# Two output tiles' gate products moved into the retention and its norms, with two score banks and four buffers there

## The chip, the cores and the metric

The kernel runs on one core of one Trainium2 chip. The metric is the device time of one launch in microseconds (us). TensorE is called PE here, VectorE DVE, ScalarE ACT, GpSimd POOL and SyncE SP, as in the profile; PEld is TensorE's weight load.

## The reference, cut to what matters

Two blocks of two layers each run on x of 512 tokens by 1024 features, all in f32. The change is in the mixer of the second block, once in each of its two layers:

```
h = rmsnorm(x, g);  proj = h @ w_in          # q, k, v of attention and retention, conv parts, gate_pre (3 x 1024)
o_da  = rmsnorm(diff_attention(...)) * (1 - lam_init)
o_ret = rmsnorm(retention(rq, rk, rv)) * silu(r_g)      # 4 heads of 64, decay matrix per head
o_sc  = sc_b * causal_dwconv(sc_c * sc_x)
gates = sigmoid(gate_pre + b_gate)                       # 3 gates per feature
y = gates[0]*(o_da @ w_da) + gates[1]*(o_ret @ w_ret) + gates[2]*(o_sc @ w_sc)
x = x + y @ w_out
```

The gates need only h, which is there from the start of the mixer; the branch products need o_da, o_ret and o_sc.

## The kernel before, in words

Activations lie transposed, features on the 128 partitions and the 512 tokens along the free axis, so that a tensor of 1024 features is 8 tiles of 128x512. `k.tile(n)` is one such tile in SBUF, `k.bank(b)` one of the 8 banks of PSUM, each 128x512. A weight **unit** is 8 blocks of 128x128. It comes from memory into a ring (three slots of two units each, L296 on SP's queue), ACT copies it to a rounded high half `w_hi` (`split_hi`, L312) and DVE subtracts to get the low half `w_lo` (`split_lo`, L320). `product` multiplies a unit with h in three passes (hi by hi, hi by lo, lo by hi: L339, L340, L341), 24 matmuls of 128x512. Both halves are buffered for `AHEAD` = 3 units: the halves of unit n+3 can be made only when PE is done with unit n, which it reports with `unit_used`.

There is no scheduler at run time. A `Work` has one function per engine and a number of ticks; a schedule is a list of (work, tick), and every engine walks the same list in order and issues what the work has for it. Engines are tied by semaphores alone, and an instruction that waits holds all that stands behind it on its engine. `behind(lead, followers)` places a follower's tick after the lead's tick that its rule names.

The stretch of the change, in each of the two layers, is this list:

- `turn_tiles`: PE transposes the retention's two value tiles (L1778), ACT copies them.
- `retention`: 16 units u = (head, block s), with 512, 384, 256 and 128 columns for s = 0 to 3. In tick u PE makes the scores of unit u (L1802) into bank 2 + u mod 4 and then the output of unit u-2 (L1810); DVE multiplies the scores with the decay matrix into one of eight buffers (L1819, "the decay" below). Scores of unit u wait for the decay of unit u-4, the output of u-2 for the decay of u-2. ACT copies each pair of heads when it is complete (L1826).
- `short_conv`, ticks behind the retention's at u = 0, 2, 4, 6: three DVE instructions (L1853 to L1856) in each of its ticks 1 and 2.
- `diff_norms` (a `tile_norms` of four tiles), ticks behind u = 3, 7, 11, 15 and one at the end: ACT squares tile n (L1736), PE averages the square (L1729), ACT takes the root in tick n+1 (L1741, Sqrt), DVE makes the reciprocal (L1756) and scales (L1757).
- `ret_norms` (the same for the retention's two tiles, after all of it, since its first square waits for all four `diff_norms`): with a Tanh on ACT (L1738) and two more DVE instructions for the silu gate (L1762, L1763).
- `gated_branches`, 2 ticks for each of the 8 output tiles d. First ACT and DVE split the eight source tiles into halves (L1904, and `split_tiles_lo`, L556). An even tick makes three gate units into banks 2 to 4: DVE multiplies with the norm factor (L1925), ACT takes tanh (L1910), DVE makes 0.5 t + 0.5 (L1928). The odd tick makes the three branch products of one unit, 24 matmuls (L1890 to L1892), into banks 5 to 7, which DVE multiplies with the gates (L1932) and adds up (L1935, L1936).

Of the kernel before, what the change touches and what calls it, by code (L numbers as in the profile page):

```python
# [35 lines left out]
P = 128  # L36
# [16 lines left out]
SEMS = (72, 58)  # L53
# [109 lines left out]
FFN_PARTS = [6, 5]  # L163

# [1625 lines left out]
def retention(k, q, key, val, buf, values_turned):  # L1790


    scores_done, decayed, out_done, copied = (k.sem() for _ in range(4))
    units = [(h, s) for h in range(4) for s in range(TB)]
    U = len(units)

    def tensor(pe, u):
        if u < U:
            h, s = units[u]
            if u >= 4:  # L1800
                pe.wait_ge(decayed, u - 3)
            pe.matmul(k.bank(2 + u % 4)[:, 0:T - s * P], key[h // 2][HALF[h % 2], s * P:(s + 1) * P],  # L1802
                      q[h // 2][HALF[h % 2], s * P:T], start=True, stop=True).then_inc(scores_done, 1)
        if u >= 2:
            v = u - 2
            h, s = units[v]
            if v == 0:
                pe.wait_ge(values_turned, 2)
            pe.wait_ge(decayed, v + 1)
            pe.matmul(k.bank(6 + h // 2)[HALF[h % 2], s * P:T], val[h // 2][:, s * P + 64 * (h % 2):s * P + 64 * (h % 2) + 64],  # L1810
                      buf[v % 8][:, 0:T - s * P], start=(s == 0), stop=(s == TB - 1)).then_inc(out_done, 1)

    def vector(dve, u):
        if u < U:
            h, s = units[u]
            dve.wait_ge(scores_done, u + 1)
            if u >= 8:
                dve.wait_ge(out_done, u - 7)
            dve.tensor_tensor(buf[u % 8][:, 0:T - s * P], k.c(f"decay{h}")[:, 0:T - s * P],  # L1819
                              k.bank(2 + u % 4)[:, 0:T - s * P], ALU.mult).then_inc(decayed, 1)  # L1820

    def scalar(act, u):
        if u in (9, U + 1):
            j = 0 if u == 9 else 1
            act.wait_ge(out_done, 8 * (j + 1))
            act.activation(q[j], k.bank(6 + j), ACT.Copy).then_inc(copied, 1)  # L1826

    w = Work(U + 2, tensor, scalar, vector)
    w.copied, w.out_done = copied, out_done
    return w  # L1830
# [33 lines left out]
def gated_branches(k, l, first, h, factor, src, src_ready, branch, out, gt, part):  # L1864
# [5 lines left out]
    ks = [range(0, 4), range(4, 6), range(6, 8)]  # L1870

    def tensor(pe, t):
        d = t // 2
        n = first + 4 * d
        if t % 2 == 0:
            for b in range(3):
                if d >= 1:
                    pe.wait_ge(tanh_done, 3 * (d - 1) + b + 1)
                k.product(pe, k.bank(2 + b), n + b, h)
            return  # L1880
        if d >= 1:
            pe.wait_ge(read, 3 * d)
        pe.wait_ge(k.lo_ready, n + 4)
        if d == 0:
            pe.wait_ge(src_lo, DT)
        u = (n + 3) % AHEAD
        for b in range(3):
            for i in ks[b]:
                w, end = slice(i * P, (i + 1) * P), i == ks[b][-1]
                pe.matmul(k.bank(5 + b), k.w_hi[:, u, w], branch.hi(i), start=(i == ks[b][0]), stop=False)  # L1890
                pe.matmul(k.bank(5 + b), k.w_hi[:, u, w], branch.lo(i), start=False, stop=False)  # L1891
                last = pe.matmul(k.bank(5 + b), k.w_lo[:, u, w], branch.hi(i), start=False, stop=end)  # L1892
        last.then_inc(k.unit_used, 1)

    def scalar(act, t):
        d = t // 2
        n = first + 4 * d
        if t % 2:
            k.split_hi(act, n + 3 + AHEAD)
            return  # L1900
# [4 lines left out]
        else:  # L1905
            act.wait_ge(read, 3 * d)
        for b in range(3):
            k.split_hi(act, n + b + AHEAD)
            act.wait_ge(scaled, 3 * d + b + 1)
# [5 lines left out]
    def vector(dve, t):  # L1915
        d = t // 2
        n = first + 4 * d
# [4 lines left out]
        if t % 2 == 0:  # L1922
            for b in range(3):
# [3 lines left out]
            dve.wait_ge(tanh_done, 3 * (d + 1))  # L1927
            ch.then(dve.tensor_scalar(gt, gt, 0.5, 0.5, ALU.mult, ALU.add))  # L1928
            return
        dve.wait_ge(k.unit_used, n + 4)  # L1930
        for b in range(3):
            dve.tensor_tensor(part[b], gt[:, b * T:(b + 1) * T], k.bank(5 + b), ALU.mult).then_inc(read, 1)  # L1932
        k.split_lo(dve, n + 3 + AHEAD)
# [212 lines left out]
def second_block(k, l, n, act, up, const_in, lam_in, bias_dram, out):  # L2146
# [78 lines left out]
    ret = retention(k, tiles(12, 14), tiles(14, 16), tiles(16, 18), tiles(4, 12), turn.copied)  # L2225
# [17 lines left out]
    def src_ready(act, i):  # L2243
# [4 lines left out]
        else:  # L2248
            act.wait_ge(conv.done, i - 5)

    gates = gated_branches(k, l, n, h, rstd, tiles(0, 4) + tiles(12, 14) + tiles(20, 22), src_ready,
                           k.halves(28, DT), tiles(4, 12), k.tile(14, 3), tiles(17, 20))
    schedule = ticks(turn) + behind(ret, [(conv, lambda u: 2 * u), (diff_norms, lambda u: 4 * u + 3)])
# [14 lines left out]
    schedule += ticks(ret_norms) + gate_ticks[:-1] + splits[:-1] + gate_ticks[-1:] + splits[-1:] + ticks(o.early)  # L2268
# [28 lines left out]
def pack_weights(i):  # L2297
# [26 lines left out]
    for l in range(DEPTH):  # L2324
# [4 lines left out]
        for d in range(DT):  # L2329
            g += [unit(w[:, 3328 + b * D + d * P:3328 + b * D + (d + 1) * P]) for b in range(3)]  # L2330
            g.append(unit(branch[:, d * P:(d + 1) * P]))
# [68 lines left out]
```

## Time and profile before

| | |
|---|---|
| median of 3 runs | 3365.84 us (3365.09 to 3366.28) |
| time of the profiled execution | 3363.61 us |
| its span, from first to last instruction | 3361.8 us |
| PE busy | 3212.4 us (96%) |
| DVE, ACT, POOL busy | 54%, 35%, 5% |
| mean granted TensorE clock | 0.975 |

Rows of a timeline give start, duration, engine, line and operation, the number of instructions merged (x), and in square brackets how long the engine sat idle before, with what released it. A PE matmul's duration overlaps the next one's, so the pace is read from start to start. A matmul of f32 tiles that are not split shows as two instructions.

### The profile page before, as it was taken

The numbers are of one execution on the slowest core, as the hardware profiler recorded it, in microseconds if no ns is written. First come the engines' busy times: TensorE is split into PE (matmuls) and PEld (weight loads), VectorE is DVE, ScalarE is ACT, GpSimd is POOL, SyncE is SP. The second block draws the span as 40 slices with busy tenths as digits, with TensorE's granted clock in tenths as the row PEclk, the third lists the DMA queues.
The fourth block names the chain that finished last, engine by engine and source line by source line (L and its number), as shares of the span: only waits on it lengthen the run. The fifth ranks groups of instructions, "written<-read, shape, count | busy, mean of one in ns | idle before, by whom it ended". The sixth has DMA issues, their size and how long they took to land.

```text
span 3361.8 us, 42275 instructions
## 1 busy us (share of the span) xinstructions
PE 3212.4 (96%) x17384; PEld 2531.6 (75%) x17384; DVE 1821.2 (54%) x2794; ACT 1162.8 (35%) x1813; POOL 157.1 (5%) x129
## 2 busy tenths in 40 slices
PE   9999899999899889999899899999999999999999
PEld 6778778887677667888677587788877757778887
DVE  3854443343677754333476755564647675556463
ACT  4533233232433334222343323432335332333232
POOL 1221000000000010000000000100010000010000
PEclk9999889999999988999899999999999999999999
DMA  4210012222111111222211122223222112222322
GB/s 173 76 40 19 15 63 100 88 100 96 50 63 63 63 63 63 89 99 88 96 63 64 37 100 88 97 79 108 91 94 87 63 38 100 88 88 87 108 82 81
DMA packets 41563, 264.89 MB, mean 79 GB/s; under 512 B 4600, under 2 KB 4984, under 8 KB 13980
## 3 DMA queue, kind: packets, MB, share of 16 engines
q1 hardware_dynamic: 41364, 262.18, 22.9%
q8 instruction: 138, 2.26, 0.3%
q14 instruction: 53, 0.43, 0.0%
q10 hardware_dynamic: 8, 0.01, 0.0%
HBM read 260.07 MB, written 3.42 MB: 78 GB/s over the span
## 4 chain that ended last, share of the span: by engine, by line
PE 75%; DVE 9%; ACT 3%; issue 2%; DVEq 0%; ACTq 0%; POOL 0%; POOLq 0%
PE psum L339 22%; PE psum L340 22%; PE psum L341 22%; PE psum L757 2%; DVE w_lo L320 1%; PE psum L943 1%; ACT tiles L964 1%; PE psum L934 1%; DVE tiles L989 1%; DVE tiles L1694 1%; PE psum L1890 1%; PE psum L1891 1%; PE psum L1892 1%; ACT xT L818 1%; PE psum L1802 1%
## 5 line engine op out<-in xcount | busy, mean ns | idle before, releaser
L339 PE MATMUL psum<-hi,w_hi 128*128 128x512 f32 x3672 | 1477.1, 402 | 33.5 <-DVE lo L799 15.3
L340 PE MATMUL psum<-lo,w_hi 128*128 128x512 f32 x3672 | 1456.7, 397 | 0.0
L341 PE MATMUL psum<-hi,w_lo 128*128 128x512 f32 x3672 | 1455.7, 396 | 0.0
L339 PEld LDWEIGHTS psum<-hi,w_hi 128*128 128x128 f32 x3672 | 692.7, 189 | 216.1 <-issue 16.1
L320 DVE TENSOR_TENSOR w_lo<-ring,w_hi 128x1024 fp32r<-128x1024 f32 (+1 forms) x495 | 602.9, 1218 | 427.1 <-ACT w_hi L312 426.8
L312 ACT ACTIVATE w_hi<-ring 128x1024 fp32r<-128x1024 f32 (+1 forms) x495 | 505.3, 1021 | 941.3 <-PE psum L341 880.5
L340 PEld LDWEIGHTS psum<-lo,w_hi 128*128 128x128 f32 x3672 | 693.4, 189 | 169.8 <-issue 6.1
L341 PEld LDWEIGHTS psum<-hi,w_lo 128*128 128x128 f32 x3672 | 692.4, 189 | 169.6
L730 DVE SCALAR_TENSOR_TENSOR xT<-xT,psum 128x512 f32<-128x512 f32 x96 | 66.0, 688 | 240.3 <-PE psum L341 240.3
L964 ACT ACTIVATE tiles<-tiles,small 128x256 f32<-128x256 f32 (+3 forms) x176 | 95.0, 541 | 147.3 <-DVE small L989 146.6
L1570 DVE TENSOR_TENSOR tiles<-tiles 128x512 f32<-128x512 f32 x64 | 44.3, 693 | 180.6 <-ACT tiles L1562 180.6
L1562 ACT ACTIVATE tiles<-psum 128x512 f32<-128x512 f32 x64 | 38.2, 597 | 224.7 <-PE psum L341 224.7
L934 PE MATMUL psum<-tiles 128*128 128x256 f32 (+3 forms) x352 | 107.2, 432 | 0.0
L943 PEld LDWEIGHTS psum<-tiles 128*128 128x128 f32 x400 | 53.3, 194 | 67.0 <-issue 49.1
L943 PE MATMUL psum<-tiles 128*128 128x128 f32 x400 | 63.4, 290 | 40.4 <-DVE tiles L976 35.0
L957 ACT ACTIVATE tiles<-psum 128x128 f32<-128x128 f32 (+1 forms) x80 | 34.9, 436 | 178.1 <-PE psum L925 177.9
L1925 DVE TENSOR_TENSOR psum<-psum,tiles 128x512 f32<-128x512 f32 x48 | 33.6, 699 | 107.5 <-PE psum L341 107.4
L989 DVE CUSTOM_DVE_ANT_0 tiles<-psum,tiles 128x128 f32<-128x128 f32 (+3 forms) x96 | 44.8, 485 | 64.0 <-PE psum L934 63.5
L1237 PE MATMUL psum<-tiles 64*64 64x64 f32 x2496 | 78.8, 219 | 0.5 <-DVE tiles L1393 0.5
L1237 PEld LDWEIGHTS psum<-tiles 64*64 64x64 f32 x2496 | 75.3, 135 | 3.6 <-issue 1.7
L934 PEld LDWEIGHTS psum<-tiles 128*128 128x128 f32 x352 | 59.3, 199 | 22.6 <-issue 14.4
L744 POOL TENSOR_TENSOR tiles<-tiles 128x512 f32<-128x512 f32 x18 | 31.3, 1739 | 847.4 <-ACT tiles L716 847.4
(249 smaller groups left out, 2612.2 us busy)
## 6 DMA issues: line engine op xcount, KB each, us to landing
ring<-in_weights SPq DMA_DIRECT2D x211, 1024.0 KB, 4.8
ring<-in_weights SPq DMA_DIRECT2D x28, 704.0 KB, 4.0
ring<-in_weights SPq DMA_DIRECT2D x4, 896.0 KB, 4.5
ring<-in_weights SPq DMA_DIRECT2D x3, 832.0 KB, 4.4
xT<-in_x SPq DMA_DIRECT2D x8, 256.0 KB, 5.4
tiles<-bias_repeated SPq DMA_DIRECT2D x8, 256.0 KB, 7.2
out<-xT SPq DMA_DIRECT2D x8, 256.0 KB, 2.8
held<-in_const SPq DMA_DIRECT2D x1, 1344.0 KB, 7.7
```

Source lines behind the costliest of these rows:

```text
L312: act.activation(self.w_hi[:, n % AHEAD, 0:UNITS[n] * P], self.raw(n), ACT.Copy).then_inc(self.hi_ready, 1)
L320: dve.tensor_tensor(self.w_lo[:, n % AHEAD, w], self.raw(n), self.w_hi[:, n % AHEAD, w].bitcast(F32), ALU.subtract).then_inc(self.lo_ready, 1)
L339: pe.matmul(out, hi, rhs.hi(first + at), start=(at == 0), stop=False)
L340: pe.matmul(out, hi, rhs.lo(first + at), start=False, stop=False)
L341: last = pe.matmul(out, lo, rhs.hi(first + at), start=False, stop=(at == end))
L730: dve.scalar_tensor_tensor(out=k.x(t), in0=k.x(t), scalar=scale, in1=k.bank(t % nb), op0=ALU.mult, op1=ALU.add).then_inc(added, 1)
L757: ins = pe.matmul(out[:, i * w:(i + 1) * w], src[:, i * P:(i + 1) * P], weights, start=first and i == 0, stop=last and i == TB - 1)
L934: pe.matmul(s_bank[g][:, lo:hi], q[:, i * P:(i + 1) * P], key[:, lo:hi], start=True, stop=True).then_inc(scores_done, 1)
L943: last = pe.matmul(o_bank[:, 0:P], heads[h][1][:, b], probT[:, b], start=(j == 0), stop=(j == i))
L964: act.activation(prob[g][:, lo:hi], prob[g][:, lo:hi], ACT.Exp, bias=s[:, top:top + 1], scale=-1.0, accum_out=s[:, 3 + g:4 + g]).then_inc( ...
L989: dve.tensor_tensor_reduce(out=prob[g][:, span], in0=s_bank[g][:, span], in1=bias[:, end - ((i + 1) * P - first(i)):end], scale=-scale, sc ...
L1237: last = pe.matmul(out[HALF[h], to], left[HALF[h], at_chunk(c)], right[HALF[h], at_chunk(c)], start=True, stop=True)
```

## The change

The first two output tiles' six gate units become a `Work` of their own, `early_gates`, with tiles to keep the results in and banks 4 and 5. Its ticks 0 to 3 stand behind the retention's ticks 2, 6, 10 and 14, ticks 4 and 5 between the ticks of `ret_norms`. To free banks and tiles the retention keeps two score banks and four decay buffers. `gated_branches` begins with the branch products of tiles 0 and 1, one behind the other, and makes gates from tile 2 on. The weights are packed in the new order (six gate units, two branch units, then three and one as before); their number and size stay. The lengths of the two pools of semaphores go from 72 and 58 to 74 and 56.

```
@@ retention, tensor
-            if u >= 4:
-                pe.wait_ge(decayed, u - 3)
-            pe.matmul(k.bank(2 + u % 4)[:, 0:T - s * P], key[h // 2][HALF[h % 2], s * P:(s + 1) * P],
+            if u >= 2:
+                pe.wait_ge(decayed, u - 1)
+            pe.matmul(k.bank(2 + u % 2)[:, 0:T - s * P], key[h // 2][HALF[h % 2], s * P:(s + 1) * P],
@@ retention, vector
-            if u >= 8:
-                dve.wait_ge(out_done, u - 7)
-            dve.tensor_tensor(buf[u % 8][:, 0:T - s * P], k.c(f"decay{h}")[:, 0:T - s * P],
-                              k.bank(2 + u % 4)[:, 0:T - s * P], ALU.mult).then_inc(decayed, 1)
+            if u >= 4:
+                dve.wait_ge(out_done, u - 3)
+            dve.tensor_tensor(buf[u % 4][:, 0:T - s * P], k.c(f"decay{h}")[:, 0:T - s * P],
+                              k.bank(2 + u % 2)[:, 0:T - s * P], ALU.mult).then_inc(decayed, 1)
@@ new
+def early_gates(k, l, first, h, factor, gates, banks, tile_free):
+    scaled, tanh_done, made = (k.sem() for _ in range(3))
+
+    def tensor(pe, e):
+        if e >= 2:
+            pe.wait_ge(tanh_done, e - 1)
+        k.product(pe, k.bank(banks[e % 2]), first + e, h)
+
+    def scalar(act, e):
+        d, b = e // 3, e % 3
+        k.split_hi(act, first + e + AHEAD)
+        tile_free(act, e)
+        act.wait_ge(scaled, e + 1)
+        act.activation(gates[e], k.bank(banks[e % 2]), ACT.Tanh, scale=0.5,
+                       bias=k.v("b_gate", 24 * l + 8 * b + d)).then_inc(tanh_done, 1)
+
+    def vector(dve, e):
+        dve.wait_ge(k.unit_used, first + e + 1)
+        dve.tensor_tensor(k.bank(banks[e % 2]), k.bank(banks[e % 2]), factor, ALU.mult).then_inc(scaled, 1)
+        k.split_lo(dve, first + e + AHEAD)
+        dve.wait_ge(tanh_done, e + 1)
+        dve.tensor_scalar(gates[e], gates[e], 0.5, 0.5, ALU.mult, ALU.add).then_inc(made, 1)
@@ gated_branches, tensor (odd tick, branch products)
         if d >= 1:
             pe.wait_ge(read, 3 * d)
-        pe.wait_ge(k.lo_ready, n + 4)
+        pe.wait_ge(k.lo_ready, n + 1)
         if d == 0:
             pe.wait_ge(src_lo, DT)
+            pe.wait_ge(early.tanh_done, 3 * EARLY_GATES)
@@ gated_branches, scalar and vector: no gates for d < EARLY_GATES; vector, odd tick
+        if d == 0:
+            dve.wait_ge(early.made, 3 * EARLY_GATES)
         for b in range(3):
-            dve.tensor_tensor(part[b], gt[:, b * T:(b + 1) * T], k.bank(5 + b), ALU.mult).then_inc(read, 1)
+            gate = gates[3 * d + b] if d < EARLY_GATES else gt[:, b * T:(b + 1) * T]
+            dve.tensor_tensor(part[b], gate, k.bank(5 + b), ALU.mult).then_inc(read, 1)
@@ second_block
+    held = tiles(8, 12) + [k.tile(62), k.tile(22)]
+    early = early_gates(k, l, n, h, rstd, held, (4, 5), tile_free)
-    schedule = ticks(turn) + behind(ret, [(conv, lambda u: 2 * u), (diff_norms, lambda u: 4 * u + 3)])
+    schedule = ticks(turn) + behind(ret, [(conv, lambda u: 2 * u), (diff_norms, lambda u: 4 * u + 3),
+                                          (early, lambda e: 2 + 4 * e if e < 4 else T)])
-    schedule += ticks(ret_norms) + gate_ticks[:-1] + splits[:-1] + gate_ticks[-1:] + splits[-1:] + ticks(o.early)
+    schedule += [(ret_norms, 0), first_gates[4], (ret_norms, 1), first_gates[5], (ret_norms, 2)] + gate_ticks[:-1] + splits[:-1] + gate_ticks[-1:] + splits[-1:] + ticks(o.early)
```

Lines of the changed kernel stand one further down than before until the retention's end. The rows that follow are instructions in the order in which an engine holds them; a stage semaphore has a number only.

DVE in the first layer's retention, from unit 7's decay on, before (`stage0_6` is the scores' semaphore, `stage0_8` the outputs', `stage0_12` the norms' root on ACT, `stage0_14` DVE's own):

```order
L1819 TENSOR_TENSOR tiles<-held,psum 128x128 [waits stage0_6]
L1756 RECIPROCAL tiles<-tiles 128x512 [waits stage0_12]
L1757 SCALAR_TENSOR_TENSOR tiles<-tiles,small 128x512 [waits stage0_14]
L1819 TENSOR_TENSOR tiles<-held,psum 128x512 [waits stage0_8,stage0_6]
L1819 TENSOR_TENSOR tiles<-held,psum 128x384 [waits stage0_8,stage0_6]
L1819 TENSOR_TENSOR tiles<-held,psum 128x256 [waits stage0_8,stage0_6]
```

The same engine in the changed kernel, from unit 8's decay on (L1895 is the scaling of early gate 2, `stage0_23` its tanh):

```order
L1820 TENSOR_TENSOR tiles<-held,psum 128x512 [waits stage0_8,stage0_6]
L1820 TENSOR_TENSOR tiles<-held,psum 128x384 [waits stage0_8,stage0_6]
L1820 TENSOR_TENSOR tiles<-held,psum 128x256 [waits stage0_8,stage0_6]
L1895 TENSOR_TENSOR psum<-psum,tiles 128x512 [waits unit_used]
L321 TENSOR_TENSOR w_lo<-ring,w_hi 128x1024 [waits hi_ready]
L1898 TENSOR_SCALAR tiles<-tiles 128x512 [waits stage0_23]
L1820 TENSOR_TENSOR tiles<-held,psum 128x128 [waits stage0_8,stage0_6]
L1757 RECIPROCAL tiles<-tiles 128x512 [waits stage0_12]
L1758 SCALAR_TENSOR_TENSOR tiles<-tiles,small 128x512 [waits stage0_14]
L1820 TENSOR_TENSOR tiles<-tiles,psum 128x512 [waits stage0_8,stage0_6]
```

Between the 256-column and the 128-column decay of a head now stand three instructions of an early gate, the first of which waits for the end of its product on PE; the norm's reciprocal and the next head's first decay stand behind them.

ACT over the same units, before (L1826 copies the first two heads, L1736 squares, L1741 takes roots):

```order
L1826 ACTIVATE tiles<-psum 128x512 [waits stage0_8]
L1736 ACTIVATE tiles<-tiles 128x512 [waits stage0_15]
L1741 ACTIVATE tiles<-psum,common 128x512 [waits stage0_11]
L1736 ACTIVATE tiles<-tiles 128x512 [waits stage0_15]
L1741 ACTIVATE tiles<-psum,common 128x512 [waits stage0_11]
```

And in the changed kernel (L1890 is the early gates' tanh, `stage0_22` their scaling on DVE):

```order
L313 ACTIVATE w_hi<-ring 128x1024 [waits unit_used,slot_filled2]
L1890 ACT_TABLE_LOAD
L1890 ACTIVATE tiles<-psum,vec 128x512 [waits stage0_22]
L1737 ACTIVATE tiles<-tiles 128x512 [waits stage0_15]
L1742 ACT_TABLE_LOAD
L1742 ACTIVATE tiles<-psum,common 128x512 [waits stage0_11]
```

A weight split and a tanh now stand ahead of each square and root, and a table load ahead of each change between tanh and root; this group of six stands there for early gates 2 and 3.

DVE ahead of the split of the source tiles, before:

```order
L1756 RECIPROCAL tiles<-tiles 128x512 [waits stage0_18]
L1757 SCALAR_TENSOR_TENSOR tiles<-tiles,vec 128x512 [waits stage0_20]
L1762 SCALAR_TENSOR_TENSOR tiles<-tiles 128x512 [waits stage0_19]
L1763 SCALAR_TENSOR_TENSOR tiles<-tiles 128x512 [waits stage0_20]
L556 TENSOR_TENSOR lo_4893<-tiles,hi_4892 128x512 [waits stage0_22] x8
L1925 TENSOR_TENSOR psum<-psum,tiles 128x512 [waits unit_used]
```

And in the changed kernel, from early gate 5 on:

```order
L1895 TENSOR_TENSOR psum<-psum,tiles 128x512 [waits unit_used]
L321 TENSOR_TENSOR w_lo<-ring,w_hi 128x1024 [waits hi_ready]
L1898 TENSOR_SCALAR tiles<-tiles 128x512 [waits stage0_23]
L1757 RECIPROCAL tiles<-tiles 128x512 [waits stage0_18]
L1758 SCALAR_TENSOR_TENSOR tiles<-tiles,vec 128x512 [waits stage0_20]
L1763 SCALAR_TENSOR_TENSOR tiles<-tiles 128x512 [waits stage0_19]
L1764 SCALAR_TENSOR_TENSOR tiles<-tiles 128x512 [waits stage0_20]
L557 TENSOR_TENSOR lo_4895<-tiles,hi_4894 128x512 [waits stage0_25] x8
```

The second norm and the eight splits, which before stood behind nothing that needed a gate product, now stand behind the last early gate, and no gate product is left on PE between them and the first branch product.

## Rows read from the trace of the kernel before

**Rows 1.** Head of the page.

```profile
span 3361.8 us, 42275 instructions
```

**Rows 2.** Windows: length, PE, PEld, DVE, ACT, POOL busy, PEclk, DMA share, GB/s.

```profile
1876.36:1903.74 27.38, 27.38 (x82) 10.00 (x80) 23.02 (x33) 7.10 (x11) 4.84 (x4) 1.00 0.12 39
1903.74:1932.83 29.09, 21.81 (x78) 15.37 (x77) 23.12 (x23) 15.06 (x22) 0.00 (x0) 0.82 0.00 1
...
2719.57:2776.04 56.47, 49.14 (x159) 25.32 (x157) 46.15 (x55) 22.17 (x33) 4.84 (x4) 0.91 0.06 19
```

**Rows 3.** Timeline of PE, first layer's retention to branch products.

```profile
1880.46 0.49 PE L1802 MATMUL psum<-tiles 64*128 64x128 f32 x2
...
1887.18 0.48 PE L1802 MATMUL psum<-tiles 64*128 64x128 f32 x2
...
1888.38 1.12 PE L1729 MATMUL psum<-tiles,held 128*128 128x512 f32 x2
1889.44 1.12 PE L1802 MATMUL psum<-tiles 64*128 64x512 f32 x2
...
1892.27 0.70 PE L1802 MATMUL psum<-tiles 64*128 64x256 f32 x2
...
1893.90 0.48 PE L1802 MATMUL psum<-tiles 64*128 64x128 f32 x2
...
1910.30 2.08 PE L1729 MATMUL psum<-tiles,common 128*128 128x512 f32 x2 [6.56 <-ACT tiles L1736]
...
1955.33 0.40 PE L1890 MATMUL psum<-hi,w_hi 128*128 128x512 f32 x1
```

**Rows 4.** Timeline of DVE, first layer.

```profile
1887.91 3.35 DVE L1756 RECIPROCAL tiles<-tiles 128x512 f32<-128x512 f32 x1
...
1891.96 1.48 DVE L1819 TENSOR_TENSOR tiles<-held,psum 128x512 f32<-128x512 f32 x3
...
1908.78 0.75 DVE L1757 SCALAR_TENSOR_TENSOR tiles<-tiles,small 128x512 f32<-128x512 f32 x1
1915.26 3.35 DVE L1756 RECIPROCAL tiles<-tiles 128x512 f32<-128x512 f32 x1 [5.73 <-ACT tiles L1741]
...
1926.02 4.90 DVE L556 TENSOR_TENSOR lo<-tiles,hi 128x512 fp32r<-128x512 f32 x8
...
1938.80 1.88 DVE L1932 TENSOR_TENSOR tiles<-tiles,psum 128x512 f32<-128x512 f32 x3 [1.62 <-PE psum L1892]
```

**Rows 5.** Timeline of ACT, first layer.

```profile
1912.09 0.61 ACT L1736 ACTIVATE tiles<-tiles 128x512 f32<-128x512 f32 x1
1912.61 0.61 ACT L1738 ACTIVATE tiles<-tiles 128x512 f32<-128x512 f32 x1
1913.24 1.28 ACT L1741 ACT_TABLE_LOAD   x1
1914.54 1.26 ACT L1741 ACTIVATE tiles<-psum,common 128x512 f32<-128x512 f32 x2
...
1949.99 1.06 ACT L312 ACTIVATE w_hi<-ring 128x1024 fp32r<-128x1024 f32 x1 [3.94 <-PE psum L341]
1950.95 0.67 ACT L1910 ACTIVATE tiles<-psum,vec 128x512 f32<-128x512 f32 x1
1955.59 1.06 ACT L312 ACTIVATE w_hi<-ring 128x1024 fp32r<-128x1024 f32 x1 [3.97 <-PE psum L341]
```

**Rows 6.** Timeline of PE around two other waits.

```profile
911.46 0.68 PE L943 MATMUL psum<-tiles 128*128 128x128 f32 x4 [2.14 <-DVE tiles L976]
...
1779.56 0.72 PE L943 MATMUL psum<-tiles 128*128 128x128 f32 x4 [3.54 <-DVE tiles L976]
```

**Rows 7.** Windows behind the waits of rows 6 and 3, columns as in rows 2.

```profile
1910.30:1916.60 6.30, 5.92 (x9) 2.92 (x10) 1.34 (x1) 6.26 (x9) 0.00 (x0) 0.50 0.00 0
1780.00:1783.40 3.40, 3.40 (x11) 2.73 (x10) 2.43 (x8) 2.17 (x5) 0.00 (x0) 0.51 0.00 0
...
911.00:916.00 5.00, 4.54 (x22) 3.80 (x23) 2.81 (x12) 2.77 (x8) 0.00 (x0) 1.00 0.26 110
```

## What was predicted

> **What bounds the kernel now.** I read the head of the page first: a span of 3361.8 us [rows 1]; the execution took 3363.6 us, 2.2 us less than the median of the runs, 3365.8. Then windows over the stretch that the change touches, in both layers. From the turn of the values to the first branch product the first layer needs 27.4 + 29.1 = 56.5 us, the second as long [rows 2]. The first part, turn and retention, is PE's: busy 27.38 of 27.38 us [rows 2]. So a gate product put there does not fill a hole, it lengthens the part by its own 5.6 us (the pace of the weight splits, 1949.99 to 1955.59 [rows 5]). But DVE is busy there too, 23.0 of 27.4 us, with reciprocals of 3.35 us between the decays [rows 2, 4], and PE can pass them only because its scores run four units ahead. The second part is where PE loses: it waits 6.56 us for the first square of `ret_norms` [rows 3] and then runs at the granted clock of 0.50, the 1.2 GHz level, for 6.3 us [rows 7]. Its work there is two norm matmuls of 1.06 us and three products of 5.6, together 18.9, so 29.1 - 18.9 = 10.2 us per layer is all that the change can win. DVE is busy 23.1 of these 29.1 us [rows 2]: the second norm ends and the eight source splits begin at 1926.02 and last 4.9 us, and the branch product at 1932.83 comes just behind them [rows 4, 2]. The three gate products are the cover of that DVE work.
>
> **The change, step by step.** The mechanism that decides is DVE's order. The scaling of early gate e stands ahead of the last decay of its head, and waits for the whole product. Behind it are the weight split, the gate's 0.5 t + 0.5, the decay, then the norm's reciprocal and only then the next head's first decay. With two score banks PE cannot start unit u before the decay of u-2, so the next product can't start before that first decay is done. I count from P, the moment PE could start the instruction behind a product.
>
> The leg behind early gates 2 and 3: ACT begins 0.26 us after P (1955.33 to 1955.59 [rows 3, 5]) and splits for 1.06; a table load, 1.30 to the next start; tanh at 2.62; 0.52 to the square at 3.14, 0.63 to the next load at 3.77, 1.30 to the root at 5.07, 0.72 to DVE's reciprocal at 5.8 [rows 4, 5]. From its start to the next decay are 4.05 us (1887.91 to 1891.96 [rows 4]): 9.84. That decay is about 0.7 (512 of the 1152 columns of 1.48 us [rows 4] give 0.66), so PE goes on at 10.6. A unit of 256 columns with its output takes 1.63 (1892.27 to 1893.90 [rows 3]), and the next product starts at 12.2 and ends at **17.8**. Without waits it would be 1887.18 to 1893.90 = 6.7 [rows 3] plus 5.6 = 12.3.
>
> The other periods, each from the end of one product to the end of the next:
> - Turn to P0: 1876.36 to 1880.46 is 4.1 [rows 2, 3], plus 5.6: **9.7**.
> - P0 to P1: no reciprocal yet. Tanh at 0.26 + 0.96 [rows 5] = 1.22, square 1.74, its 0.61 and a lag of 0.07 to PE's norm matmul at 2.4, then 1.06 + 2.83 + 1.63 (1888.38, 1889.44, 1892.27, 1893.90 [rows 3]) + 5.6: **13.5**. The convolution's DVE instructions lie beside PE's waits and cost nothing; with that cover gone they would add 2 us.
> - P1 to P2: as the leg above, but ACT holds tanh's table, 1.4 less: **16.4**.
> - P2 to P3: **17.8**.
> - P3 to P4: no next head. Two reciprocals follow, the second at 9.84, the last scaling at 9.84 + 3.38 = 13.2, and from there to PE's norm matmul 1908.78 to 1910.30 = 1.52 [rows 4, 3]: 14.7. PE was done at about 6, so it waits 9 us, longer than the 6.56 of before, and comes back at the 1.2 GHz level: 2.08 for the norm matmul [rows 3], to 16.8, and the rest of 6.3 slow us, 4.2, does 2.1 of the 5.6 [rows 7]; 3.5 more ends at about **24.5**.
> - P4 to P5: the second square waits behind gate 4's tanh: norm matmul at 2.4, + 1.06 + 5.6 = **9.1**. DVE's first retention norm starts at 1.74 + 0.52 + 0.63 + 1.30 + 0.72 = 4.9 and needs 5.38 (half of 1915.26 to 1926.02 [rows 4]), to 10.3, which is P5 + 1.2.
> - P5 to branch 0: scaling at 1.2 to 1.9, load, tanh at 3.2, load 3.8, root 5.1, reciprocal 5.85, 5.38 to 11.2, eight splits 4.9 [rows 4] to 16.1. PE has nothing to do in all of this: **16.2**.
>
> The sum is 9.7 + 13.5 + 16.4 + 17.8 + 24.5 + 9.1 + 16.2 = 107.2 us. Three more products than before are done by then, 16.8 us which the steady part is spared: 90.4 against 56.5, **+33.9**. Then come costs behind it. Branch product 0 runs after a wait of 16 us; the slow spells in the rows last 3.4 and 6.3 us [rows 7] and half of one is lost, 1.7 to 3.1: I take 2.4. Branch product 1 stands right behind it and waits for DVE to read banks 5 to 7: 0.26 + 1.88 [rows 3, 4] + 0.05 = 2.2, which before lay under gate products. Last, the clock in the new short waits: by the periods above PE stops for 2.9 (before P2), 2.6 and 2.9 (P3), 2.6 (P4), 2.4 (P5) and 2.2 us (branch 1). A wait of 2.14 us left the granted clock at 1.00, one of 3.54 was followed by 3.4 us at 0.51, a loss of 1.7 [rows 6, 7]. Six waits between them cost 0 to 10.2; I take half, 5. That is 33.9 + 2.4 + 2.2 + 5 = 43.5 per layer, 87 for both. The span goes from 3361.8 to 3449, the execution to 3451, the median to **3453**.
>
> At nothing I cost the new order of the weights (same units, same groups, asked for at a slower pace than before, with a DMA share of 0.12 and 0.00 in these windows [rows 2]), the four decay buffers (a buffer's output, unit u-4, is issued two units earlier on PE) and the copies of L1826, which ACT makes between a root and the next split while PE runs a product. If a ring slot were late it would delay a split behind it; the pace leaves 11 us per slot.
>
> ACT's table switches: four per layer in this stretch before, ten now, and eight lie on the chain above (one behind gate 1, two each behind 2 and 3, one behind 4, two behind 5). A load is 1.28 us, the root starts 1.30 after it, and the instruction ahead of it is followed by the load as soon as its own 0.61 is over [rows 5]. The sum has them at that price, 10.4 us per layer. The Trainium skill, "ScalarE: Activation LUTs", section "What ACT_TABLE_LOAD costs", gives 1.28 us for the load and 1.38 more for draining, 2.66 for each switch; by that the sum would be 8 x 1.38 x 2 = 22 us higher, 3475. The rows show no such drain here, so I keep theirs.
>
> **The rivals.**
> - *Faster.* The gates fill PE's waits and DVE keeps pace: 2 x 10.2 us won, 3345. For it: PE truly stands idle 6.56 us and runs slow [rows 3, 7]. It decides where the way from the turn to branch 0 takes less than 56.5 + 16.8 = 73.3 us, and I get 107. DVE alone is busy 23.0 + 23.1 [rows 2], and gets three more gates at about 0.7 + 1.2 + 0.5, so it would have to lose under 20 us in waits for six products of 5.6. 3 in 100.
> - *The last wait is covered.* DVE has its norms done early enough that the 16.2 us before branch 0 and the slow clock behind it vanish: 43.5 - 16.2 - 2.4 = 24.9 per layer, 3416. Against it stands the fixed order, norm and splits behind gate 5. 8 in 100.
> - *A table switch costs more than its row.* If each of the eight held ACT as long again as the 1.30 us of the rows [rows 5], 8 x 1.3 x 2 = 21 us, 3474. 6 in 100. It is the case that the Trainium skill's page on ScalarE's tables would have.
> - *The clock stays low through the stretch.* If each of the six short waits brings a spell of 6.3 us [rows 7], 19 instead of 5 per layer, 3481. 5 in 100.
> - *No change.* The waits fall where PE was waiting anyway. 2 in 100, since PE was busy all through the retention.
>
> **How the numbers follow.** The chain as worked out has 76 in 100, with 3425 to 3470 as its own range: the clock terms at their lower ends take off 2 x (5 + 0.7), at their upper ends add 2 x (5.2 + 0.7), and some 10 us either way are for steps of the walk that are off by a few tenths each. The range 3410 to 3488 takes in the covered wait below and the two cases above. Slower 95, faster 3, within 0.2% (6.7 us, about what a measurement can tell) 2 in 100.
>
> **What the profile would show.** Right: PE idle 8 to 9 us before the first retention norm matmul and about 16 before branch product 0; waits of 2 to 3 us before tick 10's and 14's scores, released by DVE's decay; DVE idle 4 to 5 us before each L1895, released by PE; six more table loads per layer; a turn-to-branch window of 105 to 115 us; the same pace from tile 2 on. It is wrong if the decay behind a reciprocal does not release PE, if ACT's squares and roots run ahead of the tanh, or if the granted clock stays at 1.00 through the waits.

## The result, and the profile after

The changed kernel takes 3456.7 us (median of 4 runs, 3450.1 to 3458.9) against 3365.5; the ratio is 1.0271, with an interval of 1.0255 to 1.0286. It is 91 us slower, where 3453 was forecast. Of the ten runs of the kernel `both` below one took 8040 us; its ratio leaves that run out, and no trace explains it.

The page of the changed kernel, its head and its line of busy times:

```profile
span 3455.1 us, 42303 instructions
...
PE 3240.3 (94%) x17384; PEld 2545.8 (74%) x17384; DVE 1823.2 (53%) x2802; ACT 1178.9 (34%) x1825; POOL 156.8 (5%) x129
```

PE has the same 17384 instructions and is busy 28 us longer, since matmuls take longer where the granted clock is lower; the span grew by 93.3. The rest of the growth is waiting. The two layers show the same pattern; the rows below are the first layer's.

The timeline of PE in the changed kernel, the lines that answer to [rows 3]; a line without brackets had no wait ahead of it:

```profile
1888.22 0.49 PE L1803 MATMUL psum<-tiles 64*128 64x128 f32 x2
...
1890.59 1.12 PE L1730 MATMUL psum<-tiles,held 128*128 128x512 f32 x2 [1.10 <-ACT tiles L1737]
...
1901.90 0.48 PE L1803 MATMUL psum<-tiles 64*128 64x128 f32 x2
...
1911.04 0.73 PE L1803 MATMUL psum<-tiles 64*128 64x256 f32 x2 [2.81 <-DVE tiles L1820]
...
1920.01 0.48 PE L1803 MATMUL psum<-tiles 64*128 64x128 f32 x2
...
1923.80 1.13 PE L1730 MATMUL psum<-tiles,held 128*128 128x512 f32 x2 [2.52 <-ACT tiles L1737]
...
1930.57 1.22 PE L1803 MATMUL psum<-tiles 64*128 64x256 f32 x2 [0.74 <-DVE tiles L1820]
...
1940.22 0.48 PE L1803 MATMUL psum<-tiles 64*128 64x128 f32 x2
...
1954.94 2.08 PE L1730 MATMUL psum<-tiles,common 128*128 128x512 f32 x2 [9.01 <-ACT tiles L1737]
...
1966.03 1.96 PE L1730 MATMUL psum<-tiles,common 128*128 128x512 f32 x2 [2.30 <-ACT tiles L1737]
...
1989.95 0.77 PE L1937 MATMUL psum<-hi,w_hi 128*128 128x512 f32 x1 [15.57 <-DVE lo L557]
...
1999.38 0.50 PE L1937 MATMUL psum<-hi,w_hi 128*128 128x512 f32 x1 [1.98 <-DVE tiles L1985]
```

Each line of 128 columns of L1803 is the first instruction behind an early product, so the ends of products 0 to 3 are 1888.22, 1901.90, 1920.01 and 1940.22. Product 4 ends at 1966.03 - 2.30 = 1963.73 and product 5 at 1989.95 - 15.57 = 1974.38. What DVE did in the leg behind early gate 2, to set beside [rows 4]:

```profile
1920.11 0.70 DVE L1895 TENSOR_TENSOR psum<-psum,tiles 128x512 f32<-128x512 f32 x1 [7.89 <-PE psum L342]
1921.26 1.23 DVE L321 TENSOR_TENSOR w_lo<-ring,w_hi 128x1024 fp32r<-128x1024 f32 x1 [0.45 <-ACT w_hi L313]
1923.26 0.43 DVE L1898 TENSOR_SCALAR tiles<-tiles 128x512 f32<-128x512 f32 x1 [0.77 <-ACT tiles L1890]
1923.60 0.28 DVE L1820 TENSOR_TENSOR tiles<-held,psum 128x128 f32<-128x128 f32 x1
1925.78 3.35 DVE L1757 RECIPROCAL tiles<-tiles 128x512 f32<-128x512 f32 x1 [1.90 <-ACT tiles L1742]
...
1929.83 1.15 DVE L1820 TENSOR_TENSOR tiles<-tiles,psum 128x512 f32<-128x512 f32 x2
```

DVE stands still for 7.89 us until the product is over, and then PE waits in turn for what DVE has to do: reciprocal at 5.8 us behind the product, decay at 9.8, as worked out. ACT in the same leg, to set beside [rows 5]:

```profile
1920.17 1.06 ACT L313 ACTIVATE w_hi<-ring 128x1024 fp32r<-128x1024 f32 x1 [11.31 <-PE psum L342]
1921.25 1.28 ACT L1890 ACT_TABLE_LOAD   x1
1922.54 0.69 ACT L1890 ACTIVATE tiles<-psum,vec 128x512 f32<-128x512 f32 x1
1923.13 0.62 ACT L1737 ACTIVATE tiles<-tiles 128x512 f32<-128x512 f32 x1
1923.76 1.28 ACT L1742 ACT_TABLE_LOAD   x1
1925.06 0.69 ACT L1742 ACTIVATE tiles<-psum,common 128x512 f32<-128x512 f32 x1
```

Windows of the changed kernel from product to product, with the columns of [rows 2]:

```profile
1888.22:1901.90 13.68, 12.58 (x44) 6.66 (x43) 6.42 (x14) 2.15 (x3) 1.29 (x1) 1.00 0.00 0
1901.90:1920.01 18.11, 14.20 (x44) 7.25 (x43) 8.04 (x9) 4.72 (x6) 0.00 (x0) 0.91 0.17 58
1920.01:1940.22 20.21, 16.95 (x43) 7.99 (x43) 8.13 (x9) 5.51 (x6) 0.00 (x0) 0.75 0.00 1
1940.22:1963.73 23.51, 11.98 (x37) 7.28 (x36) 10.66 (x8) 9.23 (x11) 0.00 (x0) 0.78 0.13 45
1963.73:1974.38 10.65, 8.35 (x27) 5.67 (x26) 7.66 (x7) 4.64 (x6) 0.00 (x0) 0.84 0.00 0
1974.38:1989.95 15.57, 0.00 (x1) 0.03 (x1) 12.56 (x15) 9.26 (x13) 0.00 (x0) 0.57 0.19 67
1989.95:2006.61 16.66, 14.69 (x48) 11.38 (x49) 4.31 (x6) 1.06 (x1) 0.00 (x0) 0.79 0.00 1
```

The first column is the length of each period, the seventh the granted clock. From the turn to the first branch product are 112.0 us in the first layer and 113.8 in the second, against 56.5 in both before; three gate products more are done by then in each. The parts add up to the growth of the span: 55.6 + 57.3 in the two stretches, 9.9 and 11.3 less in what follows them (three products of 5.6 fewer, less what the two branch products lose), and 1.6 more ahead of the first.

### The profile page after: what moved, and what is told of

It is laid out like the page before. It is cut to its first block, busy times and chain, and to the rows that moved or that the text cites. A ratio compares the mean times of both kernels' runs of the same rounds, so it can differ in the third digit from the quotient of the medians.

```text
span 3455.1 us, 42303 instructions
## 1 busy us (share of the span) xinstructions
PE 3240.3 (94%) x17384; PEld 2545.8 (74%) x17384; DVE 1823.2 (53%) x2802; ACT 1178.9 (34%) x1825; POOL 156.8 (5%) x129
## 4 chain that ended last, share of the span: by engine, by line
PE 75%; DVE 8%; ACT 4%; issue 2%; DVEq 0%; ACTq 0%; POOL 0%; POOLq 0%
PE psum L340 22%; PE psum L342 22%; PE psum L341 22%; PE psum L758 2%; DVE w_lo L321 1%; PE psum L944 1%; PE psum L935 1%; ACT tiles L965 1%; PE psum L1937 1%; PE psum L1938 1%; PE psum L1939 1%; DVE tiles L1695 1%; DVE tiles L990 1%; ACT xT L819 1%; ACT w_hi L313 1%
## 5 line engine op out<-in xcount | busy, mean ns | idle before, releaser
L340 PE MATMUL psum<-hi,w_hi 128*128 128x512 f32 x3672 | 1484.1, 404 | 32.4 <-DVE lo L800 14.0
L1937 PE MATMUL psum<-hi,w_hi 128*128 128x512 f32 x128 | 53.5, 418 | 35.1 <-DVE lo L557 31.1
L935 PEld LDWEIGHTS psum<-tiles 128*128 128x128 f32 x352 | 59.2, 198 | 22.5 <-issue 14.3
L1974 DVE TENSOR_TENSOR psum<-psum,tiles 128x512 f32<-128x512 f32 x36 | 25.2, 699 | 92.2 <-PE psum L342 92.2
```

Of the source, the lines that this page charges most:

```text
L340: pe.matmul(out, hi, rhs.hi(first + at), start=(at == 0), stop=False)
L935: pe.matmul(s_bank[g][:, lo:hi], q[:, i * P:(i + 1) * P], key[:, lo:hi], start=True, stop=True).then_inc(scores_done, 1)
```

## The experiments

The table has the stretch from the turn to the first branch product, read from each profile's PE timeline, beside the time. All ratios are to runs of the kernel before that were made beside the kernel in question; their medians lie between 3364.1 and 3365.5, so that a ratio can differ a little from that of the two medians shown.

| kernel | median us | ratio, interval | stretch, layers 1 and 2 (us) |
|---|---|---|---|
| before | 3365.5 | | 56.5, 56.5 |
| changed | 3456.7 | 1.0271, 1.0255 to 1.0286 | 112.0, 113.8 |
| banks | 3366.8 | 1.0008, 0.9997 to 1.0018 | 57.7, 57.7 |
| late_rest | 3424.7 | 1.0175, 1.0160 to 1.0191 | 97.7, 97.3 |
| no_tanh | 3428.2 | 1.0188, 1.0173 to 1.0203 | 102.6, 101.4 |
| after_sources | 3450.5 | 1.0261, 1.0239 to 1.0283 | 108.4, 110.3 |
| pe_fill | 3370.8 | 1.0021, 1.0011 to 1.0030 | 56.5, 56.5 |
| short_chain | 3361.9 | 0.9993, 0.9983 to 1.0002 | 54.0, 55.1 |
| both | 3357.7 | 0.9978, 0.9968 to 0.9987 | 50.8, 50.8 |
| both_ahead | 3352.1 | 0.9967, 0.9956 to 0.9979 | 50.2, 50.2 |
| pool_splits | 3347.4 | 0.9951, 0.9936 to 0.9966 | 50.1, 50.0 |

The theory was that of the prediction: DVE's place in the list, ahead of the reciprocal and the next head's decay, makes PE and DVE wait for each other in turn, and the last products no longer cover DVE's chain. The rivals were the banks, the table loads, and PE's own load.

### banks

```
-            if u >= 4:
-                pe.wait_ge(decayed, u - 3)
-            pe.matmul(k.bank(2 + u % 4)...
+            if u >= 2:
+                pe.wait_ge(decayed, u - 1)
+            pe.matmul(k.bank(2 + u % 2)...
```

and the buffers 8 to 4, in the kernel before.

> The kernel before with one part of the change alone: two score banks and four decay buffers, no early gates. Theory (the gates' place in DVE's order costs the time, the banks next to nothing): PE waits 0.4 us in the first units and about 0.5 at each head whose first decay stands behind a reciprocal, 1.5 to 2 us per layer, 3369 us (3367 to 3371). Rival (the banks make PE wait for DVE at every unit and carry a good part of the 91 us): 3385 or more.

3366.8 us; the stretch is 1.2 us longer in each layer. The timeline of PE has two small waits that were not there before, besides the one ahead of the branch product:

```profile
1895.14 0.70 PE L1802 MATMUL psum<-tiles 64*128 64x256 f32 x2 [0.35 <-DVE tiles L1819]
1902.28 0.70 PE L1802 MATMUL psum<-tiles 64*128 64x256 f32 x2 [0.35 <-DVE tiles L1819]
```

The first scores take 0.4 us longer too (2.60 for 2.20). By themselves two banks and four buffers cost next to nothing: 1.2 us, where the stretch of the changed kernel grew by 55.5, and an interval of the ratio that includes 1. Beside early gates they may cost more, for with four banks PE could run further ahead of the late decay; no kernel with early gates and four banks was run.

### late_rest

In the changed kernel, `early_gates` is cut in two works, the products and the rest:

```
-    w = Work(3 * EARLY_GATES, tensor, scalar, vector)
+    w = Work(3 * EARLY_GATES, tensor)
+    w.rest = Work(3 * EARLY_GATES, scalar=scalar, vector=vector)
...
-                                          (early, lambda e: 2 + 4 * e if e < 4 else T)])
+                                          (early, lambda e: 2 + 4 * e if e < 4 else T),
+                                          (early.rest, lambda e: 4 + 4 * e if e < 4 else T)])
```

Ticks 4 and 5 keep products and rest together where they were.

> The changed kernel with its products where they are, but what DVE and ACT do for early gates 0 to 3 (scaling, weight split, tanh, 0.5 t + 0.5) set behind the next head's first decay, ticks 4, 8, 12 and 16 of the retention. Theory (DVE's wait for the product, ahead of reciprocal and decay, sets each period): a reciprocal starts 0.8 us behind a product and not 4.2 to 5.8, so the periods of 13.7, 18.1 and 20.2 us become 12.3, 12.8 and 12.8, with no clock loss, 15 to 16 us per layer, 3425 us (3419 to 3431). Rival (the six products cost PE time in a part where PE was full, wherever DVE's share stands): within 5 us of 3457.

3424.7 us, 32 less than the changed kernel. The timeline of DVE behind product 2, which ended at 1913.66:

```profile
1914.18 0.29 DVE L1820 TENSOR_TENSOR tiles<-held,psum 128x128 f32<-128x128 f32 x1 [5.12 <-PE psum L1803]
1914.39 3.35 DVE L1757 RECIPROCAL tiles<-tiles 128x512 f32<-128x512 f32 x1
...
1918.44 0.68 DVE L1820 TENSOR_TENSOR tiles<-tiles,psum 128x512 f32<-128x512 f32 x1
1919.03 0.69 DVE L1895 TENSOR_TENSOR psum<-psum,tiles 128x512 f32<-128x512 f32 x1
```

The reciprocal starts 0.7 us behind the product and not 5.8, and PE waits 0.35 us ahead of the unit of 256 columns. Products 0 to 3 end at 1888.22, 1900.74, 1913.66 and 1926.59: periods of 12.5, 12.9 and 12.9 us, where 12.3, 12.8 and 12.8 were expected. The products are the same and PE's order is the same, so in these three periods their place on PE costs little beyond their own 5.6 us each; DVE's and ACT's order does. It is 14.3 and 16.5 us per layer, of the 38.7 and 40.5 by which the changed kernel's stretches exceed 56.5 us and three products of 5.6. The rest stands as it did: the wait of 15.57 us ahead of the branch products, and the period from product 3 to 4, 22.9 us here and 23.5 before, in which PE now waits 10.49 us for the first square of the retention's norms. The order of the follow-ups does not touch these, and no run tries the second of them by itself.

### no_tanh

```
-        act.activation(gates[e], k.bank(banks[e % 2]), ACT.Tanh, scale=0.5,
+        act.activation(gates[e], k.bank(banks[e % 2]), ACT.Identity, scale=0.5,
```

> The changed kernel with ACT's Identity in place of Tanh for the six early gates, so that these gates have wrong values (a part of the computation is changed) and six of the ten table loads per layer are gone. Theory (loads lie on the chain at the 1.30 us of their rows): 2.6 us less in each of the three legs with two loads, 15.6 in all, and 0 to 6 more where a shorter wait keeps the clock up, 3438 us (3434 to 3442). Rival 1 (a switch costs 2.6 to 2.7 us with its drain): 32 less, 3425. Rival 2 (the loads are hidden in PE's waits): no change, 3457.

3428.2 us, 28 less than the changed kernel, and so past the expected 18 and near the first rival's 32. The trace tells the two apart. The ACT timeline has the leg behind early gate 2 without loads:

```profile
1918.69 1.06 ACT L313 ACTIVATE w_hi<-ring 128x1024 fp32r<-128x1024 f32 x1 [11.34 <-PE psum L342]
1919.65 0.67 ACT L1890 ACTIVATE tiles<-psum,vec 128x512 f32<-128x512 f32 x1
1920.22 0.62 ACT L1737 ACTIVATE tiles<-tiles 128x512 f32<-128x512 f32 x1
1920.74 0.68 ACT L1742 ACTIVATE tiles<-psum,common 128x512 f32<-128x512 f32 x1
```

The root starts 2.05 us behind the split and not 4.89, so two loads cost 2.84, 1.4 each with the lag at each change, and no drain of another 1.38 each. By the product ends 1900.38, 1918.53 and 1935.22 and the first branch product at 1979.06, the three legs with loads are shorter by 3.5, 3.2 and 2.5; the stretch is 9.4 us shorter in the first layer and 12.3 in the second. The two stretches give 21.7 us, of which the loads explain 6 x 1.4 x 2 = 17; the rest of these is put down to the clock (its mean over the stretches is 0.88 against 0.82), which no run separates. Of the other 7 us between the two profiled spans, 1.5 lie ahead of the first stretch and 5.2 between the stretches, where nothing was changed: from the first branch product to the next turn are 771.7 us against 776.9. The last section shows what that is. So the rival's total was nearly met and its cause is not there.

### after_sources

In the changed kernel, ACT's copies and DVE's subtractions for source tiles 0, 1, 6, 7, 2 and 3 become ticks of their own:

```
-    schedule += [(ret_norms, 0), first_gates[4], ...
+    schedule += [(ret_norms, 0)] + ticks(gates.sources) + [first_gates[4], ...
```

> The changed kernel with the splits of six of the eight source tiles moved from behind the last early gate to behind the first retention square, where DVE waits 9.6 us for a gate product and ACT 7.0. Theory (nothing covers DVE's chain ahead of the first branch product in the changed kernel, so what leaves it comes off in full): 6 x 0.61 us, the wait of 15.6 us becomes 11.9, 7 us in all, 3449 us (3446 to 3453). Rival (the first branch product waits for the last early gate's tanh or weight split as long): no change, 3457.

3450.5 us, 6 less than the changed kernel. The PE timeline:

```profile
1986.34 0.76 PE L1946 MATMUL psum<-hi,w_hi 128*128 128x512 f32 x1 [12.14 <-DVE lo L1916]
```

The wait of 15.57 is 12.14 and the stretches are 3.6 and 3.5 us shorter, six subtractions' worth. What leaves DVE's chain behind the last early gate comes off in full: nothing covers it in the changed kernel. This shows it for 3.5 of the 15.57 us; that the other 12 go the same way is argued from the chain, not tried.

### pe_fill

In the kernel before, gate product 0 moves on PE alone:

```
+    w.filler = Work(1, lambda pe, t: k.product(pe, k.bank(2), first, h))
...
-    schedule += ticks(ret_norms) + gate_ticks[:-1] ...
+    schedule += ticks(gates.filler) + ticks(ret_norms) + gate_ticks[:-1] ...
```

> The kernel before with the first gate product moved on PE alone into its wait of 6.56 us ahead of the retention's norms; nothing moves on DVE or ACT. Theory (in the second part DVE's chain of reciprocals and splits sets the start of the first branch product, so that filling PE wins nothing): the branch product starts within 0.3 us of where it did, PE waits some 6 us just ahead of it and the branch product runs at the lower clock, 2 to 3 us lost per layer: 3370 us (3365 to 3372). Rival (the wait and the slow clock are PE's to win, 5 to 9 us per layer): 3348 to 3355.

3370.8 us, 0.2% slower, with an interval that leaves out 1. The PE timeline, against [rows 3]:

```profile
1912.86 1.12 PE L1729 MATMUL psum<-tiles,common 128*128 128x512 f32 x2 [0.76 <-ACT tiles L1736]
...
1935.39 0.80 PE L1892 MATMUL psum<-hi,w_hi 128*128 128x512 f32 x1 [6.16 <-DVE w_lo L320]
```

The wait ahead of the norms goes from 6.56 to 0.76 us, and all of it comes back as 6.16 us ahead of the branch product; the stretch is 56.5 us to the tenth. The idle time that the change set out from was never PE's to win alone.

### short_chain, both, both_ahead, pool_splits

These start from the kernel before. short_chain sets the two tanh of the retention's norms behind both roots and splits six source tiles ahead of the norms:

```
+        if n == N and tanh_last:
+            for m in range(N):
+                act.activation(th[m], jobs[m][4], ACT.Tanh, scale=0.5).then_inc(tanh_done, 1)
...
-    schedule += ticks(ret_norms) + gate_ticks[:-1] ...
+    sources = ticks(gates.sources)
+    schedule += sources[:5] + [(ret_norms, 0), sources[5]] + ticks(ret_norms)[1:] + gate_ticks[:-1] ...
```

> The kernel before with DVE's and ACT's chain ahead of the first branch product shortened and PE's order untouched: the two tanh of the retention's norms behind both roots (one table load less ahead of the first reciprocal), and the splits of six of the eight source tiles moved from behind the norms into DVE's wait of 5.7 us ahead of them. Theory (the second part is bound twice, by DVE's chain and, 0.3 us behind it, by PE's own order of norms and three products): PE's products now set the start of the branch product, 0 to 1 us per layer, 3363 us (3361 to 3366). Rival (DVE's chain alone is the bound): 5 us per layer, 3354.

3361.9 us, a ratio that includes 1; the stretch is 2.5 and 1.3 us shorter, more than the 0 to 1 expected. PE has no wait left ahead of the branch product, as the theory has it. About 1 us of the excess is that the two norm matmuls now run one behind the other; the rest was not followed up.

both adds `ticks(gates.filler)` of pe_fill ahead of `sources[:5]`.

> As short_chain, and the first gate product moved on PE into its wait ahead of the norms, as in pe_fill. Theory: only together do they win. PE is done with the three products at 1923.6 on the clock of the profile before, DVE lets the branch product start at 1927.0 and not 1932.8; a wait of 3.4 us that may bring a slow spell of 1.7 us: 4 to 6 us per layer, 3354 us (3351 to 3358). Rival (the parts win what each does alone, about 0 and a loss): 3364 to 3370.

3357.7 us. The stretch is 50.8 us, 5.6 less, where 50.6 was worked out; pe_fill alone gave 0 and short_chain 2. PE waits as foretold:

```profile
1928.32 0.80 PE L1904 MATMUL psum<-hi,w_hi 128*128 128x512 f32 x1 [3.53 <-DVE w_lo L321]
```

and its first instructions behind that wait take 0.80 us, not 0.40, so some 2 us of each gain are given back (the branch product takes 7.1 us in the first layer and 8.3 in the second, for 5.7); the median's gain, 7 us, is at the lower end of what was expected.

both_ahead takes the split of the fourth gate unit off the end of the chain:

```
-    schedule += ... [(ret_norms, 0), sources[5]] + ...
+    schedule += ... [(ret_norms, 0), sources[5], (gates.ahead, 0)] + ...
```

> As both, with ACT's and DVE's split of the fourth gate unit made in DVE's wait and not behind the last source split. Theory: it takes 0.6 us of DVE's chain, the branch product starts at 1926.4: 3353 us (3349 to 3356). Rival (a split ahead of the norms delays the first root and the reciprocals behind it): slower than both by 2 us or more.

3352.1 us, stretch 50.2, 0.6 less as expected; the wait ahead of the branch product is 1.95 us in the first layer and 0.34 in the second, and the product behind it takes 7.2 and 5.7 us. The stretches explain 1.3 of the 5.6 us between the medians of this kernel and both, whose intervals overlap.

pool_splits gives four of the six early subtractions to POOL:

```
-    w.sources = Work(6, None, early_hi, lambda dve, n: source_lo(dve, n, FIRST_SOURCES[n]))
+    w.sources = Work(6, None, early_hi, lambda dve, n: source_lo(dve, n, FIRST_SOURCES[n]) if n >= 4 else None,
+                     lambda pool, n: source_lo(pool, n, FIRST_SOURCES[n]) if n < 4 else None)
```

> As both_ahead, with the subtraction for four source tiles (two of the attention's, two of the convolution's) on POOL, which is idle. Theory: 2.4 us less on DVE's chain, the branch product starts at 1925.0, 1.4 us behind PE's last product, so that the clock stays up: 7 to 8 us per layer, 3349 us (3346 to 3353). Rival (POOL's work slows DVE's beside it, or POOL is too slow for its four splits): no faster than both_ahead.

3347.4 us, the lowest median of all, 18 us less than before, though its interval overlaps that of both_ahead. But the stretch is 50.1 and 50.0 us, only 0.1 to 0.2 less than both_ahead's and not 1.4. The timelines of POOL and of DVE, over the same microseconds:

```profile
1905.89 5.49 POOL L1878 TENSOR_TENSOR lo<-tiles,hi 128x512 fp32r<-128x512 f32 x4 [17.53 <-ACT hi L1882]
```

and

```profile
1909.11 1.14 DVE L1761 SCALAR_TENSOR_TENSOR tiles<-tiles,small 128x512 f32<-128x512 f32 x1
1910.18 2.36 DVE L1878 TENSOR_TENSOR lo<-tiles,hi 128x512 fp32r<-128x512 f32 x2
```

The scaling takes 1.14 us and not the 0.75 of [rows 4], and two subtractions 2.36, where eight took 4.90. So the rival was right in part: DVE is slowed beside POOL, and its chain ends 0.9 us earlier than in both_ahead and not 2.4. The branch product does not gain even that, for PE no longer waits ahead of it: its own norms and products, at a granted clock of 0.89 from 1911.00 to 1926.70, now end last, where the same work in both_ahead's first layer ran at 1.00. The profiled spans of the last two kernels differ by 6.0 us. Only 0.4 of that lies in the two stretches; 2.4 lie ahead of the first, where nothing was changed, and 3.2 between them, in two equal parts: the branch product that no longer follows a wait of 1.95 us and runs at full clock, and a slow spell less in the feed-forward part. So at most some 2 us can be put down to POOL's work.

## Why the prediction was right

- *The mechanism and its place.* Both held. late_rest shows that this order is the cause of the excess in the three periods up to product 3, after_sources that DVE's chain ends the last wait. DVE's waits ahead of L1895 were given as 4 to 5 us before each. They are 4.4, 5.6, 7.9, 8.1, 9.6 and 0.4 us: only the first fits, and the walk itself would have given about 6 for the third and fourth (the output of 512 columns and the product, 1.0 + 5.6, less DVE's 256-column decay). PE's slow clock made the same work some 1.6 us longer there.
- *The sum.* By period, forecast and measured: turn to P0 9.7 and 10.3; P0 to P1 13.5 and 13.7; P1 to P2 16.4 and 18.1; P2 to P3 17.8 and 20.2; P3 to P4 24.5 and 23.5; P4 to P5 9.1 and 10.6; P5 to branch 0 16.2 and 15.6. The seven add up to 107.2 and 112.0, and in the second layer to 113.8. The excess sits in the periods whose granted clock is 0.91, 0.75 and 0.84; it is the part forecast apart as "I take half, 5". That half was a choice between 0 and 10.2, and that it came out so near is partly luck, as is that P3 to P4 and P5 to branch 0, 1.0 and 0.6 us too long in the sum, took back a part of what other periods lacked. P3 to P4 is shorter since the slow spell behind the wait lasted 4.4 us (granted clock 0.50 from 1954.94 to 1959.37) and not 6.3. The instants at which DVE releases PE are off by a tenth: 9.1 us behind P1 (forecast 9.2) and 10.6 behind P2 (10.6). In the period from P2, slow matmuls filled most of PE's last wait, 0.74 us and not 2.9, so the clock's loss and the wait's are partly the same time.
- *A wait left out.* Turn to P0 is 0.6 us longer than worked out: with two banks the third score waits for the first decay, so that L1803's first group takes 2.60 us where the kernel before had 2.20, and a product takes 5.8 us from its first matmul (1882.42 to 1888.22), not 5.6. In the two shortest legs PE waits 1.10 us for the square, which is in the sum but not among the six waits.
- *Behind the stretch.* Branch product 1 waits 1.98 us (2.2), branch product 0 after 15.57 us of waiting takes 7.4 us, 1.8 over its 5.6 (2.4). Branch product 1 also runs slow, 7.2 us, which the sum had only as one of six short waits. Per layer 43.5 us were forecast, and 45.7 and 46.0 measured; the last 1.6 of the span's growth lie ahead of the first stretch, where nothing was changed.
- *The range.* The chain's own range, 3425 to 3470, does not follow from its terms: 3453 less 2 x 5.7 and 10 is 3432, and with 2 x 5.9 and 10 it is 3475. The measured 3456.7 lies in either.
- *The table loads.* The rows' price held, 1.3 to 1.4 us per switch. By the Trainium skill, "ScalarE: Activation LUTs", section "What ACT_TABLE_LOAD costs", it would have been 2.66 for each; the trace does not agree, since no_tanh shows two switches to be worth 2.84 together.
- *The cover.* The step that gate products had covered DVE's chain is borne out twice: by after_sources, where the uncovered chain sets the time, and by pe_fill, where one product less over it brings PE a wait for DVE of 6.16 us and no gain.
- *The bound of before.* "10.2 us per layer is all that the change can win" was true as a limit and too generous as a hope, since DVE's chain ended within 0.3 us of PE's work (PE waits 0.34 us ahead of the branch product in the kernel before, and 0.39 in its second layer).

## What to carry to other kernels

Work that fills a wait of one engine must bring its share for the other engines too, and where these are in order, a single instruction that waits for the filler holds everything behind it; set the follow-up behind what the main chain needs next (late_rest: 32 us of 91). Before filling an idle stretch, look for what ends it: if another engine's chain is as long, moving work on one engine alone wins nothing, and shortening the chain alone wins little, but both together won 5.6 us per layer here. Work at the end of a stretch may be the cover of another engine's tail, and moving it forward lays that tail bare.

## What the runs showed of the hardware

The granted clock behind the same short wait is not the same in every kernel. Ahead of the feed-forward part PE waits 2.08 us for DVE in all of them. The PE timeline, and the 4.5 us behind that wait with the columns of [rows 2], in the changed kernel:

```profile
2143.25 0.50 PE L340 MATMUL psum<-hi,w_hi 128*128 128x512 f32 x1 [2.08 <-DVE lo L573]
```

```profile
2143.18:2147.68 4.50, 4.43 (x12) 3.50 (x13) 4.23 (x7) 0.20 (x1) 0.00 (x0) 0.62 0.19 31
```

and in no_tanh, which is the same program in that part:

```profile
2131.84 0.50 PE L340 MATMUL psum<-hi,w_hi 128*128 128x512 f32 x1 [2.08 <-DVE lo L573]
```

```profile
2131.77:2136.27 4.50, 4.43 (x19) 3.61 (x20) 4.24 (x7) 0.20 (x1) 0.00 (x0) 1.00 0.15 24
```

The mean granted clock is 0.62 behind the one and 1.00 behind the other, with 12 and 19 matmuls in 4.5 us; the kernel before has 0.62 there too. In the attention of the second layer a wait of 3.54 us does the same. The windows from its end on, in the changed kernel and in no_tanh:

```profile
2668.44:2672.44 4.00, 4.00 (x13) 3.23 (x14) 3.03 (x10) 2.25 (x5) 0.00 (x0) 0.61 0.00 0
```

```profile
2655.49:2659.49 4.00, 4.00 (x19) 3.35 (x20) 3.03 (x10) 2.26 (x5) 0.00 (x0) 1.00 0.00 0
```

So the prediction's reading of [rows 7], that a wait of 3.54 us brings 3.4 us at 0.51, holds for that place and not for every such wait. Three spells like these, some 1.5 us each, are how no_tanh gained 5 us in a part of the program that is the same, and such spells may be behind the spread of the kernel before, whose runs lie between 3353.1 and 3367.4 us. An effect of a few us on the total is therefore to be read from the stretch it belongs to. By which rule a short wait is followed by a slow spell is not settled by these runs.

DVE's tensor operations were slower while POOL's subtractions ran, 1.14 against 0.75 us for a scaling and 2.36 against 1.47 for two subtractions (both_ahead); the reciprocal in the same microseconds, from 1905.73, took its 3.35. POOL itself took 5.49 us for four subtractions.
